# Gate products of the two PEER layers as one 256-column float32r product per token, with the gate in two exact parts

## The reference

```python
s1, i1 = lax.top_k(sc[:, :, 0], 16)          # 8 heads, 128 keys on each side
s2, i2 = lax.top_k(sc[:, :, 1], 16)
...                                          # the best 16 of the 256 sums of a head: top_s, eidx
g = softmax(top_s)                           # 8 heads x 16 experts a token
a = gelu(einsum('chkd,cd->chk', take(u, eidx), xc))
return einsum('chk,chkd->cd', g * a, take(v, eidx))
```

## Time and profile before

| | us |
|---|---|
| median of 3 runs (2506.16 to 2512.29) | 2511.76 |
| span of the profiled execution | 2506.7 |
| PE busy in the span | 2415.1 (96%) |
| DVE busy | 1745.4 (70%) |
| ACT busy | 1343.7 (54%) |
| POOL busy | 710.7 (28%) |

### The profile page before, as it was taken

How to read it: one execution, slowest core, us unless ns; L and a number is a source line. 1 busy time by engine, 2 the same in 40 slices (tenths; PEclk the granted TensorE clock), 3 DMA queues, 4 the chain that set the end, 5 groups by cost and what they waited for, 6 DMA issues and landing times. The chain is left out here.

```text
span 2506.7 us, 57329 instructions
## 1 busy us (share of the span) xinstructions
PE 2415.1 (96%) x16509; PEld 2210.5 (88%) x16509; DVE 1745.4 (70%) x3945; ACT 1343.7 (54%) x2396; POOL 710.7 (28%) x564
## 2 busy tenths in 40 slices
PE   7999999999999999999999999999999999899998
PEld 6889999999888888888999999988888887688996
DVE  5647777887777777564777788777777767556346
ACT  3545555676555555454455567665555543434443
POOL 5665444000000000566544400000000043134665
PEclk9999999999999999999999999999999999999999
DMA  6244566444566666623466644556666644432454
GB/s 242 89 145 167 211 230 225 164 155 171 186 236 245 238 243 237 244 85 138 166 217 223 229 164 152 182 175 247 234 247 236 243 161 155 144 135 105 176 189 151
DMA packets 98053, 475.31 MB, mean 190 GB/s; under 512 B 11808, under 2 KB 13344, under 8 KB 50720
## 3 DMA queue, kind: packets, MB, share of 16 engines
q1 hardware_dynamic: 97392, 472.91, 52.9%
q10 hardware_dynamic: 560, 1.19, 0.1%
HBM read 438.41 MB, written 35.65 MB: 189 GB/s over the span
## 5 line engine op out<-in xcount | busy, mean ns | idle before, releaser
L1414 ACT ACTIVATE wh<-ring 128x512 fp32r<-128x512 f32 x1428 | 882.1, 627 | 621.4 <-ACTq L1413 617.9
L2102 DVE TENSOR_TENSOR wl<-ring,wh 128x512 fp32r<-128x512 f32 x961 | 672.7, 705 | 275.0 <-DVEq L2101 257.2
L1099 PE MATMUL PS<-xh,wh 128*128 128x256 f32 x2048 | 593.9, 290 | 6.9 <-PEq L1095 5.4
L1099 PE MATMUL PS<-xl,wh 128*128 128x256 f32 x2048 | 579.9, 283 | 0.0
L1099 PE MATMUL PS<-xh,wl 128*128 128x256 f32 x2048 | 579.9, 283 | 0.0
L510 POOL TENSOR_TENSOR wl<-ring,wh 128x512 fp32r<-128x512 f32 x295 | 391.2, 1349 | 292.9 <-POOLq L509 289.4
L895 PE MATMUL PS<-wh,xh 128*128 128x512 f32 x1088 | 425.3, 391 | 2.2 <-PEq L892 2.2
L895 PE MATMUL PS<-wh,xl 128*128 128x512 f32 x1088 | 423.5, 389 | 0.0
L895 PE MATMUL PS<-wl,xh 128*128 128x512 f32 x1088 | 423.4, 389 | 0.0
L1099 PEld LDWEIGHTS PS<-xh,wh 128*128 128x128 f32 x2048 | 392.7, 192 | 12.8 <-issue 12.1
L1099 PEld LDWEIGHTS PS<-xl,wh 128*128 128x128 f32 x2048 | 393.3, 192 | 0.0
(11 more groups left out here) (339 smaller groups left out, 3817.4 us busy)
## 6 DMA issues: line engine op xcount, KB each, us to landing
ring<-in_peer_u SPq DMA_DIRECT2D x128, 1024.0 KB, 4.8
ring<-in_peer_v SPq DMA_DIRECT2D x128, 1024.0 KB, 4.8
acts<-stg SPq DMA_DIRECT2D x124, 256.0 KB, 2.1
gains<-acts SPq DMA_DIRECT2D x124, 256.0 KB, 4.9
ring<-in_w_in SPq DMA_DIRECT2D x24, 1024.0 KB, 4.9
ring<-in_w_gate_up SPq DMA_DIRECT2D x22, 1024.0 KB, 4.8
ring<-in_peer_wq SPq DMA_DIRECT2D x16, 1024.0 KB, 4.8
ring<-in_w_down SPq DMA_DIRECT2D x11, 1024.0 KB, 4.8
```

The costliest lines, as they stand in the source:

```text
L1099: last = pe.matmul(PS[:, 2 * j, 0:S], w[:, q, k * P:(k + 1) * P], x[:, at, :], start=at + i == 0, stop=at + i == 9)
L1414: act.activation(wh[:, q, :], ring[:, s, q * QW:(q + 1) * QW], ACT.Copy).then_inc(high_ready[q], 1)
L2102: part = dve.tensor_tensor(wl[:, q, :], ring[:, s, q * QW:(q + 1) * QW], wh[:, q, :].bitcast(F32), SUB)
```

## The change

A gate is cut into two parts that float32r holds exactly (`gparts`, a copy to float32r and the rest). A token's product is then one float32r product: `rowhot` (one-hot rows, without gate) against 256 columns `colhot`, 128 for the high part and 128 for the low part, into two banks for four tokens. VectorE makes `rowhot` by one comparison and waits for it, then `colhot` by four scalar_tensor_tensor of 2 x 128 elements. ScalarE copies the low halves of a group from PSUM to a packed place in `gains0`; VectorE adds them to the high halves in PSUM and writes the gate matrix to the arena (`gates_in`). The one-hots of the group after next are made behind that add. All low parts of quarters from chunk 39 on (25 chunks, 100 quarters a layer) go from VectorE to GpSimd, which waits for `picks_ready` first. The groups are spread as 3, 2, 3, 2 over four chunks, six times, and twice 2. `selT` is filled by more, smaller copies. Several small buffers (`ve2`, `rstd2`, `t16`, `p16`, `pj`, `pf`, `gsm`, `s16c`, `i16c`, `qsc`, the sinks) move into rows of `sel` and `selT`; their instructions stay.

```diff
--- before.py
+++ after.py
@@ -75,6 +75,7 @@
         wl = sb("wl", [P, 4, QW], F32R)
         xh = sb("xh", [P, KB, S], F32R)
         xl = sb("xl", [P, KB, S], F32R)
+        gains0_at = nc.sbuf_base
         gains0 = sb("gains0", [P, 2, D])
         gains1 = region(4352, 2, D)
         gains2 = region(10240, 1, D)
@@ -107,24 +106,29 @@
...
-        s16c = sb("s16c", [P, 4, TOPK])
-        qsc = sb("qsc", [P, 2 * HD + 8])
+        sel_at = nc.sbuf_base
+        sel = sb("sel", [P, 4, TT, PH * TOPK])
+        selT_at = nc.sbuf_base
+        selT = sb("selT", [P, 4, S])
+        few = sel[:, 3, :, :].rearrange("p t k -> p (t k)")
+        ve2, rstd2 = few[:, 208:228], few[:, 228:248]
+        sinksc = few[:, 248:256]
+        s16c = selT[:, 3, 0:64].rearrange("p (a k) -> p a k", a=4)
+        qsc = selT[:, 3, 128:256]
-        sel = sb("sel", [P, 3, TT, PH * TOPK])
-        selT = sb("selT", [P, 3, S])
-        ohA = gains0[:, 0, :].rearrange("p (s n k) -> p s n k", s=2, n=4)
-        ohB = gains0[:, 1, :].rearrange("p (s n k) -> p s n k", s=2, n=4)
+        rowhot = nc.alloc_sbuf_tensor_at("rowhot", [P, 2, 4, P], F32R, offset=sel_at)
+        colhot = nc.alloc_sbuf_tensor_at("colhot", [P, 2, 4, 2, P], F32R, offset=gains0_at)
+        gparts = nc.alloc_sbuf_tensor_at("gparts", [P, 2, S], F32R, offset=selT_at + 2 * S * 4)
...
@@ -641,6 +645,10 @@
                         pool.sem_inc(parts_ready[2], 1)
                         pool.sem_inc(chunk_free[s], 1)
                 pool.sem_inc(pool_lows_done, 1)
+                pool.wait_ge(picks_ready, 1)
+                pool.sem_inc(picks_ready, -1)
+                low_rest(NPAIR - N_GATE, 4)
+                pool.sem_inc(pool_lows_done, 1)
                 pool.wait_ge(dve_lows_done, 1)
                 pool.sem_inc(dve_lows_done, -1)
                 powers_of_rows()
@@ -1113,8 +1121,8 @@
                     pe.wait_ge(slot_free[2 + s], 1)
                     pe.sem_inc(slot_free[2 + s], -1)
                     for n in range(4):
-                        last = pe.matmul(PS[:, 4 + 2 * s, n * P:(n + 1) * P], ohA[:, s, n, :], ohB[:, s, n, :],
-                                         start=True, stop=True)
+                        last = pe.matmul(ps2(2 + s)[:, 2 * n * P:2 * (n + 1) * P], rowhot[:, s, n, :],
+                                         colhot[:, s, n, :, :].rearrange("p i k -> p (i k)"), start=True, stop=True)
                     last.then_inc(act_full[2 + s], 1)
 
                 with pe.Fori(0, N_GATE - 1):
@@ -1129,8 +1137,10 @@
 
                 with pe.Fori(0, 6):
                     experts((0, 1, 0))
+                    experts((1, 0))
                     experts((1, 0, 1))
-                with pe.Fori(0, 14):
+                    experts((0, 1))
+                with pe.Fori(0, 2):
                     experts((0, 1))
 
                 for s in (2, 3):
@@ -1642,30 +1652,28 @@
                         act.sem_inc(slot_free[1], 1)
                         act.sem_inc(acts_kept[s] if kept else acts_out[s], 1)
 
-                def experts(c, s, first=False, kept=False, at=None, slots=()):
+                def experts(c, s, first=False, kept=False, slots=()):
 
                     high(s, 0)
                     expert(c - 1, 1 - s, 0, first)
                     high(s, 1)
                     if slots:
-                        gates_out(at, slots[0])
+                        gate_lows(slots[0])
                     high(s, 2)
                     if len(slots) > 2:
-                        gates_out(at + 4, slots[1])
+                        gate_lows(slots[1])
                     expert(c - 1, 1 - s, 1, kept=kept)
                     high(s, 3)
                     if slots:
-                        gates_out(at + 4 * len(slots) - 4, slots[-1])
-
-                av = arena[:, :].rearrange("p (e n) -> p n e", n=S)
-
-                def gates_out(at, s):
+                        gate_lows(slots[-1])
+
+                def gate_lows(s):
 
                     act.wait_ge(act_full[2 + s], 1)
                     act.sem_inc(act_full[2 + s], -1)
-                    act.sem_inc(oneh_used[s], 1)
-                    act.activation(av[:, bass.ds(at, 4), :], PS[:, 4 + 2 * s, :].rearrange("p (n e) -> p n e", n=4),
-                                   ACT.Copy).then_inc(slot_free[2 + s], 1)
+                    act.activation(gains0[:, s, 0:4 * P].rearrange("p (n e) -> p n e", n=4),
+                                   ps2(2 + s).rearrange("p (n i e) -> p n i e", n=4, i=2)[:, :, 1, :],
+                                   ACT.Copy).then_inc(lows_out[s], 1)
 
                 experts(1, 1, True)
                 experts(2, 0, True)
@@ -1678,17 +1686,12 @@
                 experts(N_ROUTE + 1, 1)
                 experts(N_ROUTE + 2, 0)
                 with act.Fori(0, 6) as i:
-                    for k in range(2):
-                        experts(2 * i + N_GATE + 1 + k, 1 - k, at=24 * i + 12 * k, slots=(k, 1 - k, k))
-                with act.Fori(0, 6) as i:
-                    for k in range(2):
-                        experts(2 * i + N_GATE + 13 + k, 1 - k, at=16 * i + 8 * k + 144, slots=(0, 1))
-                experts(NPAIR - 1, 1, kept=True, at=S - 16, slots=(0, 1))
+                    for k, (at, slots) in enumerate(((0, (0, 1, 0)), (12, (1, 0)), (20, (1, 0, 1)), (32, (0, 1)))):
+                        experts(4 * i + N_GATE + 1 + k, 1 - k % 2, slots=slots)
+                experts(NPAIR - 1, 1, kept=True, slots=(0, 1))
                 for j in range(2):
                     expert(NPAIR - 1, 1, j, kept=True)
-                    gates_out(S - 8 + 4 * j, j)
-                act.drain().then_inc(gates_done, 1)
-                act.sem_inc(oneh_done, 1)
+                    gate_lows(j)
 
                 def cast(buf, j, first=False):
 
...
@@ -2490,50 +2493,53 @@
                 for t in range(TT):
                     dve.wait_ge(dve_full[2 + t], 1)
                     dve.sem_inc(dve_full[2 + t], -1)
-                    dve.tensor_copy(selT[:, :, t * P:(t + 1) * P],
-                                    ps2(2 + t)[:, 0:3 * P].rearrange("p (i n) -> p i n", i=3)
-                                    ).then_inc(slot_free[2 + t], 1)
+                    mine = slice(t * P, (t + 1) * P)
+                    dve.tensor_copy(selT[:, 0:2, mine], ps2(2 + t)[:, 0:2 * P].rearrange("p (i n) -> p i n", i=2))
+                    own(dve.tensor_copy(gparts[:, 0, mine], ps2(2 + t)[:, 2 * P:3 * P]))
+                    own(dve.tensor_tensor(gparts[:, 1, mine], ps2(2 + t)[:, 2 * P:3 * P],
+                                          gparts[:, 0, mine].bitcast(F32), SUB))
+                    dve.sem_inc(slot_free[2 + t], 1)
                 low(0, 3, 2)
-                own(dve.engine_nop())
+                dve.sem_inc(picks_ready, 1)
 
                 def onehots(at, s):
 
-                    dve.wait_ge(oneh_used[s], 1)
-                    dve.sem_inc(oneh_used[s], -1)
-                    dve.tensor_tensor(ohB[:, s, :, :], bc(iota[:, :].unsqueeze(1), 4, P),
-                                      bc(selT[:, 1, bass.ds(at, 4)].unsqueeze(2), 4, P), ALU.is_equal)
+                    own(dve.tensor_tensor(rowhot[:, s, :, :], bc(iota[:, :].unsqueeze(1), 4, P),
+                                          bc(selT[:, 0, bass.ds(at, 4)].unsqueeze(2), 4, P), ALU.is_equal))
                     for n in range(4):
-                        last = dve.tensor_scalar(ohA[:, s, n, :], iota[:, :], selT[:, 0, bass.ds(at + n, 1)],
-                                                 selT[:, 2, bass.ds(at + n, 1)], ALU.is_equal, MUL)
+                        last = dve.scalar_tensor_tensor(colhot[:, s, n, :, :], bc(iota[:, :].unsqueeze(1), 2, P),
+                                                        selT[:, 1, bass.ds(at + n, 1)],
+                                                        bc(gparts[:, :, bass.ds(at + n, 1)].bitcast(F32), 2, P),
+                                                        ALU.is_equal, MUL)
                     last.then_inc(oneh_ready, 1)
 
-                for s in (0, 1):
-                    dve.sem_inc(oneh_used[s], 1)
-                def lows(s, at, slots):
-
-                    low(s, 0, 2)
-                    low(s, 1, 2)
-                    onehots(at, slots[0])
-                    low(s, 2, 2)
-                    if len(slots) > 2:
-                        onehots(at + 4, slots[1])
-                    low(s, 3, 2)
-                    onehots(at + 4 * len(slots) - 4, slots[-1])
+                av = arena[:, :].rearrange("p (e n) -> p n e", n=S)
+
+                def gates_in(at, s):
+
+                    dve.wait_ge(lows_out[s], 1)
+                    dve.sem_inc(lows_out[s], -1)
+                    highs = ps2(2 + s).rearrange("p (n i e) -> p n i e", n=4, i=2)[:, :, 0, :]
+                    lows = gains0[:, s, 0:4 * P].rearrange("p (n e) -> p n e", n=4)
```

(61 more changed lines are left out.)

## The result

The changed kernel took 2696.73 us in the median of four runs (2693.81 to 2704.17), the kernel before 2512.03: a ratio of 1.0743, 95% interval 1.0723 to 1.0762. It is slower, as forecast, 23 us under the predicted 2720 and inside the range. The profiled execution took 2698.61 us, its span is 2696.5.

What follows compares the result with a forecast made beforehand. VectorE was to replace TensorE as the bound: 223 us of its own plus 84 for low parts, 307 against 206.8, about +104 a layer. 2506.7 + 208 + 5.1 = 2720 us, range 2615 to 2800.

Steps and rivals of the forecast that it cites:

- TensorE, 0.90 to 0.48 us a group: Gate stage: four 256-column products replace eight records a group, so TensorE's work falls 26.3 us a layer to 180.5.
- VectorE's group, 3.49 us: Gate stage: add 1.0, row comparison with wait 0.93, four one-hot products 1.56 us; 223 us over 64 groups.
- GpSimd's 100 low parts, 84 us: Gate stage: low parts on GpSimd hold up VectorE's two-SBUF-input instructions, 0.84 us each, 84 us a layer.
- The preview's 1.02: Convolution stage before the change: each GpSimd low part beside four scalar_tensor_tensor delayed VectorE by 1.02 us.
- the part for cover: Low parts falling in VectorE's add or idle time, 0.36 of them, hide some 0.5 us each, lowering 1.02 to 0.84.
- Entry, end and clock, +5 and +4: Gate stage's edges: +5 us for entry and end together; +4 for TensorE's half clock, nearly all hidden behind VectorE.
- Theory C: Gate stage: the lower clock makes the loss; with tiny low parts the time would stay above 2650 us.
- the term 5.1 "for what lies around" the span: Whole kernel: median run time of 2511.76 us lies 5.1 above the profiled span of 2506.7, added to the forecast.
- Rival 2: Gate stage: VectorE binds but GpSimd's low parts cost it nothing; 2504 to 2554 us, chance 0.08.
- Rival 1: Gate stage: TensorE stays the bound and shorter products gain, -26 us a layer; about 2467 us, chance 0.04.
- Rival 3: Gate stage: TensorE's clock stays at half and waits add up; 2800 to 2850 us, chance 0.08.
- Rival 4: Gate stage: 256-column products take twice as long, 31 us a layer more on TensorE, forecast's time; chance within forecast's 0.80.

Runs made afterwards that it cites:

- the index row in PSUM: The changed kernel with the row that both one-hot comparisons read copied to a free PSUM bank, low parts whole on GpSimd; 2543.98 us.
- the tiny low parts: The changed kernel with GpSimd subtracting only 8 of the 512 columns of each low part in the gate stages; 2545.03 us.

## Why the prediction was right

- **TensorE, 0.90 to 0.48 us a group.** Right: 0.47 where TensorE did not wait before the group, in every kernel, and 0.55 behind a wait. With the experts' products at 0.12 it makes 180.5 us of work in a stage of 290.2. The other 110 us are 79 us of waits inside the stage (76.5 at gate groups, 2.4 at the identity products), about 25 us of lower clock (0.085 x 290) and some 4 us for the 0.08 behind each wait.
- **VectorE's group, 3.49 us.** 3.44 alone (219.8 / 64). The add has a pitch of 0.90 where 1.0 was taken from bounds of 0.60 and 1.11; the row comparison with its wait 0.95 for 0.93; the four products 1.60 for 1.56. The value of the add worked out from the row read 64 bytes apart, 0.93, was the better one than the step toward ScalarE's (the division of that row gives 0.68 ns an element and not 0.64, so 0.95).
- **GpSimd's 100 low parts, 84 us.** The term of the sum that was mis-sized most: 70.4 and 77.1 us, 0.70 and 0.77 each, against the 0.84 taken (0.60 to 1.29). The preview's 1.02 for a low part that lies wholly beside such instructions is right: 1.03 in the sets of four above. What was too dear is the part for cover. In the trace 27% of the low parts' time lies beside an add in the first stage and 22% in the second, less than the 0.36 put for add and idle time together; but the 0.5 us taken off for each covered part was too little. 1.02 less 27% and 22% gives 0.74 and 0.80, near the measured prices; this fits a low part that costs VectorE almost nothing where it is covered, but no run isolates it. The full holding of 1.30 us that was worked out beside it from the Trainium skill (SBUF — State Buffer, Who interferes with whom) would have given 92 us more for the two layers; the measured price is lower than the forecast's own, so the rule gives who excludes whom, and the record's length is too long a price. Its other half, that VectorE with at most one SBUF input doesn't contend with GpSimd, is shown by the index row in PSUM (maximum 487 for 1620).
- **Entry, end and clock, +5 and +4.** TensorE waited 5.72 us at the first gate against 2.35 and 2.38 at the identity products against 1.37: 4.4. The sum as written leaves the +5 out, while both ends of the range count it: 223 + 84 + 4 - 206.8 is the 104; with the +5 it would be 109 and 2730 us. The clock did fall, to half, 11 and 16 times in the two stages, mean 0.91 and 0.90, but cost nothing: VectorE had no idle time that a faster TensorE would have shortened. Theory C falls with this. In the stages of the kernels under 220 us the clock was 0.99 to 1.00, in the three others above 270 us 0.90 to 0.91.
- **Sum.** Predicted +104 a layer, measured 86.8 and 93.0. VectorE's own work with entry and end was put at 223 - 206.8 = 16.2, and the tiny low parts measure 16.4 and 15.9; so of the 14 us too much, 10 are the low parts and 4 the clock. Part of the nearness is luck: the gate parts came out 28 us under the forecast, and the route stages' +7.5 and the last part's +2.4, which were not in the sum and can't be assigned, made up 10 of them. The last 5 us of the distance lie in the term 5.1 "for what lies around" the span. It was read from a span and a median of different executions; the changed kernel's profiled execution took 2698.61 us with a span of 2696.5, so 2.1 us lie around it.
- **Rivals.** Rival 2 (GpSimd beside VectorE for free) is what the index row in PSUM makes true, and it measures 2544 in its 2504 to 2554. Rival 1 is reached by no whole kernel. Rival 3 fell. Rival 4 didn't happen.

## What to carry to other kernels

Work moved to GpSimd is free to VectorE only if it doesn't read SBUF while VectorE's instructions have two inputs there; read that off the maximum of a line, not its median (479 beside 1620). One small broadcast operand put in PSUM was worth 153 us here, while moving the work was worth 0.4% at most (ratio 1.0785 with it on VectorE, 1.0743 on GpSimd). And a cheaper product pays only if the engine that prepares it holds the pace in the tightest stretch, not on average: 2.25 us against a mean of 2.8 still lost 9.0 us a stage.

## What the runs showed of the hardware

- GpSimd's memset of 512 fp32 takes 526 ns and doesn't disturb VectorE's SBUF reads at all (maximum 488 ns beside it); a subtraction of the same size that reads SBUF does (maximum 1620), and costs a fully exposed VectorE 1.02 to 1.03 us.
- VectorE's scalar_tensor_tensor with one of its two tensor inputs in PSUM and one in SBUF has the same duration as with both in SBUF (476 and 479 ns for 256 elements), and GpSimd's low parts don't stretch it (maximum 487 ns).
- Turn-taking costs both sides: GpSimd's low part had a mean of 1390 ns beside VectorE's SBUF readers and 1293 beside PSUM readers.
- An add of 512 elements with one input in PSUM takes 678 ns packed, 1063 to 1095 ns with its results 1 KB apart, and 1086 ns with results in runs of four and inputs read 512 bytes and 1 KB apart.
- Four float32r products of 256 columns cost TensorE 0.47 us among others at full clock, and 0.55 us behind a wait.
